# A two-layer streaming encoder on one core: the layer loop and the MLP loop as hardware loops, and as straight code

## The chip, the cores and the metric

The kernel runs on one core of a Trainium2 chip. The metric is the device time of one launch in microseconds (us), median of several runs. Five instruction streams run side by side: TensorE (PE, with weight loads shown apart as PEld), VectorE (DVE), ScalarE (ACT), GpSimd (POOL) and SyncE (SP), which issues the large DMAs. They meet only through semaphores.

## The reference, cut to what matters

All tensors are float32, the sequence has 256 rows, the model width is 2048, and there are two layers. Each does

```
proj = rmsnorm(x) @ w_in                 # 2048 x 4352, split into three head groups
x   += concat(A, B, C) @ w_out           # A chunked attention, B sliding window, C differential attention
x   += relu(rmsnorm(x) @ w_up)**2 @ w_down   # 2048 x 8192 and 8192 x 2048
```

Both layers compute the same with other weights; only a constant of C (`lam_init`) depends on the layer. The MLP is by far the largest part: 512 of the 720 units of weights, of up to 512 KB each.

## The kernel before, in words

**Units.** All weights are streamed once. A unit is a piece of 256 rows by 512 columns of a weight matrix, brought by one DMA on SP's queue into `raw_ring` (8 places). To keep float32 accuracy, each unit is split: ACT writes the rounded part `w_hi` (L611), DVE, or POOL for 17 units of each layer, writes the remainder `w_lo` (L783, L1152). The split parts have 4 places (`AHEAD = 4`): at step s the engines split unit s + 4 while PE works on unit s. PE multiplies each unit with the split activations in three passes, hi x hi, lo x hi, hi x lo: 12 matmuls of 512 columns in a `rows_unit` (L428 to L430), and 24 matmuls of 256 columns in an `up_unit` (L467 to L469).

**Steps.** One layer is 360 steps. Steps 0 to 71 are the projection, with the attention parts put between units by tables of step numbers; then 32 steps of `w_out`; then the MLP: 32 steps of `w_up`, three turns of a loop of 32 `w_down` steps and 32 `w_up` steps, and a last 32 steps of `w_down`. The order is written out by hand in `mix` and `mlp`, once for each engine, and `layer_steps` (L290) runs them in order.

**Loops.** Two loops are hardware loops on every engine that takes part: `Fori(0, DEPTH)` over layers (on PE it is L602, on DVE L1093) and inside it `Fori(0, LOOPS)` over the three turns (L297). Each engine has its own registers, its own branch back and no barrier with the others. Semaphores count up over the whole program, so a wait inside a loop compares with a number worked out from the loop's registers (`Place.at`). Addresses of the weights on SP are worked out in registers too (`snap`). The chain semaphores `dve_chain` and `pool_chain`, by which an engine waits for its own last instruction (`link`), are cleared at the end of each layer. `sp_passed` and `dve_passed` are counted up and waited for by nobody; each holds a wait in front of the instruction behind it.

**Who is needed at a turn's start.** The last unit of a turn is an `up_unit`, the first of the next a `rows_unit` on `ht`. That unit waits for `h_done` (the first half of the activations), for `evicted` of its bank, and for its own split. The same hand-over, in the same words, stands at the loop's entry and at its exit: four places in the two layers have no branch back, four have one.

**Rope.** POOL turns the heads of five projection chunks in each layer (L1136 to L1140); DVE normalises them afterwards (L889) and PE transposes them (L475). In those stretches DVE works through short instructions, each waiting for the one before (L795 to L804), between its splits.

Of the kernel before, what the change touches and what calls it, by code (L numbers as in the profile page):

```python
# [148 lines left out]
def encoder(nc, x_in, norm1_g, w_in, a_qnorm_g, a_knorm_g, a_rel_bias, b_qnorm_g, b_knorm_g, b_sinks, c_qnorm_g,  # L149
            c_knorm_g, c_lambda_q1, c_lambda_k1, c_lambda_q2, c_lambda_k2, c_subln_g, w_out, norm2_g, w_up, w_down,  # L150
            consts, out):
    with ExitStack() as ctx:
# [94 lines left out]
        dve_chain, pool_chain = sem("dve_chain"), sem("pool_chain")  # L247
        stored = sem("stored")

        sp_passed, dve_passed = sem("sp_passed"), sem("dve_passed")  # L250

        H_CHUNKS = 16

        class Place:
# [35 lines left out]
        def layer_steps(eng, l, do_mix, do_mlp):  # L290

            pl = Place(l)
            for s in range(UP0):
                do_mix(pl, s)
            for st in mlp_steps(UP0, ["up"]):
                do_mlp(pl, *st)
            with eng.Fori(0, LOOPS) as i:  # L297
                for st in mlp_steps(LOOP0, ["down", "up"]):
                    do_mlp(Place(l, i), *st)
            for st in mlp_steps(DOWN3, ["down"]):  # L300
                do_mlp(pl, *st)
# [29 lines left out]
        @block.sync  # L331
        def _(sp):
            def load(pl, u, w, width, offset, cols):
                at = sp.snap(offset)

                if u - RAWS in POOL_UNITS:
                    sp.wait_ge(pool_split, pl.at(len(POOL_UNITS), POOL_UNITS.index(u - RAWS) + 1))
                else:
                    sp.wait_ge(split_done, pl.at(VECTOR_SPLITS, vector_splits(u - RAWS + 1) + RAWS, LOOP_UNITS))
                sp.sem_inc(sp_passed, 1)  # L340
                sp.dma_start(raw_ring[:, u % RAWS, :, 0:cols],
                             bass.AP(w.tensor, at, [[width, P], [P * width, 2], [1, cols]])).then_inc(raw_loaded[u % RAWS], 16)

            def load_proj(pl, u, layer):
                chunk, k, cols = proj_or_out(u % UNITS)
                load(pl, u, w_in, IN_W, layer * (D * IN_W) + (k * 2 * P * IN_W + PROJ[chunk][1]), cols)

            def mix(pl, s):
                u = s + FIRST_LOADS
                if u < PU:  # L350
                    load_proj(pl, u, pl.l)
                elif u < UP0:
                    chunk, k, cols = proj_or_out(u)
                    load(pl, u, w_out, D, pl.l * (D * D) + (k * 2 * P * D + (chunk - NPROJ) * CW), cols)
                else:
                    load_up(pl, u, 0, u - UP0)
                if s == 36:
                    sp.wait_ge(ext_stored, 16)
                    at = sp.snap(pl.l * (8 * EXT) + 1 + CHUNK)

                    sp.wait_ge(maxed, pl.at(JOBS, 1))
                    sp.sem_inc(sp_passed, 1)
                    sp.dma_start(bias_t[0:CHUNK, :, CHUNK:SEQ],
                                 bass.AP(ext_dram.tensor, at, [[1, CHUNK], [EXT, 8], [1, SEQ - CHUNK]])).then_inc(bias_loaded, 16)
                    sp.dma_start(bias_t[CHUNK:P, :, :],
                                 bass.AP(ext_dram.tensor, at, [[1, CHUNK], [EXT, 8], [1, SEQ]])).then_inc(bias_loaded, 16)

            def load_up(pl, u, c, k):

                i = 0 if pl.i is None else pl.i  # L370
                col = (c + (0 if u < LOOP0 else 4)) * CW + i * (4 * CW)
                load(pl, u, w_up, D_FF, pl.l * (D * D_FF) + k * 2 * P * D_FF + col, CW)

            def load_down(pl, u, c, k, past=False):
                i = 0 if pl.i is None else pl.i
                row = (c // 4 + (2 * LOOPS if past else 0)) * (D_FF // 8) + k * 2 * P
                load(pl, u, w_down, D, pl.l * (D_FF * D) + i * (2 * (D_FF // 8) * D) + (row * D + (c % 4) * CW), CW)

            def mlp(pl, s, part, buf, c, k, n):

                u = s + FIRST_LOADS
                if part == "up":
                    n = c * UPC + k + FIRST_LOADS
                    if n < 4 * UPC:
                        load_up(pl, u, n // UPC, n % UPC)
                    elif s < LOOP0:
                        load_down(pl, u, 0, n - 4 * UPC)
                    else:
                        load_down(pl, u, 8, n - 4 * UPC)
                else:  # L390
                    n = c * 4 + k + FIRST_LOADS
                    if n < 32:
                        load_down(pl, u, n // 4, n % 4, s >= DOWN3)
                    elif s < DOWN3:
                        load_up(pl, u, 0, n - 32)
                    else:

                        load_proj(pl, u, DEPTH - 1 - pl.l)

            assert DEPTH == 2  # L400
            sp.dma_start(rows[R_G1:R_G1 + DEPTH * KT, :], norm1_g.rearrange("l (k p) -> (l k) p", p=P)).then_inc(g1_loaded, 16)
            load_x(sp, 0)
            sp.dma_start(rows[R_G2:R_G2 + DEPTH * KT, :], norm2_g.rearrange("l (k p) -> (l k) p", p=P)).then_inc(rows_loaded, 16)
            for u in range(FIRST_LOADS):
                load_proj(Place(0), u, 0)
                if u < 3:
                    load_x(sp, u + 1)
            sp.dma_start(par[:, :, SINK:SINK + 16],
                         bass.AP(b_sinks.tensor, 0, [[0, P], [16, DEPTH], [1, 16]])).then_inc(misc_loaded, 16)
            sp.dma_start(const[:, C_MASK:CONSTS], consts[:, C_MASK:CONSTS]).then_inc(const_loaded, 16)  # L410
            for n, g in enumerate((c_qnorm_g, c_knorm_g, b_knorm_g, b_qnorm_g)):
                sp.dma_start(gains[:, :, n, :], bass.AP(g.tensor, 0, [[0, P], [HD, DEPTH], [1, HD]])).then_inc(misc_loaded, 16)
            with sp.Fori(0, DEPTH) as l:
                layer_steps(sp, l, mix, mlp)
            for c in range(4):
                n = CHUNKS - 4 + c

                sp.wait_ge(evicted[n % 2], Place(DEPTH - 1).evictions(n) + 1)
                sp.dma_start(out[0, :, c * CW:(c + 1) * CW].rearrange("(r p) n -> p r n", p=P),
                             x[:, :, c * CW:(c + 1) * CW]).then_inc(stored, 16)  # L420
            sp.wait_ge(stored, 16 * 4)
# [3 lines left out]
        def _(pe):  # L425
# [170 lines left out]
            for k in range(PANELS_BEFORE):  # L596
                pe.wait_ge(x_loaded[k // 2], 16)
                transposes(x_panel(k), start_banks[k])
                if k == 1:
                    pe.wait_ge(rows_loaded, 16 * 4)  # L600
                    pe.transpose(ps_v[:, 0:ROWS], rows, const[0:ROWS, C_ID:C_ID + ROWS]).then_inc(rows_t, 1)
            with pe.Fori(0, DEPTH) as l:  # L602
                layer_steps(pe, l, mix, mlp)


# [1 line left out]
        def _(act):  # L607
# [156 lines left out]
            act.dma_start(ext_dram.rearrange("l h n -> (l h) n"), head_sq[0:DEPTH * 8, 0:EXT]).then_inc(ext_stored, 16)  # L764
            act.wait_ge(lam_dot, 1)
            act.activation(lam[:, :], lam[:, :], ACT.Exp).then_inc(lam_exp, 1)
            with act.Fori(0, DEPTH) as l:
                layer_steps(act, l, mix, mlp)


# [1 line left out]
        def _(dve):  # L772
# [118 lines left out]
            def mask_and_max(pl, j):  # L891

                dve.wait_ge(scored, pl.at(JOBS, j + 1))
                if j == 24:
                    dve.wait_ge(bias_loaded, pl.at(32, 32))
                dve.sem_inc(dve_passed, 1)
                for r, (lo, n) in enumerate(((0, P), (P, SEQ))):
                    if j < 24:
                        col = C_MASK if j < 8 or r == 0 else C_MASKB
                        add = const[:, col + SEQ - n:col + SEQ]  # L900
                    else:

                        add = bass.AP(bias_t[:, :, :].tensor, (j - 24) * SEQ + n - 1, [[8 * SEQ, P], [-1, n]])
                    first = BIG if not 8 <= j < 24 else cur[:, NSINK + j - 8:NSINK + j - 7]
                    last = dve.tensor_tensor_reduce(probs[:, j % 3, lo:lo + n], ps_s[:, lo:lo + n], add, -0.125, first,
                                                    ALU.add, ALU.min, neg_max[:, j, r:r + 1])
                last.then_inc(maxed, 1)
# [181 lines left out]
            for l in range(DEPTH):  # L1089
                link(dve.scalar_tensor_tensor(par[:, l, NLAM:NLAM + 1], lam[:, 2 * l + 1:2 * l + 2], -lam_init(l),  # L1090
                                              lam[:, 2 * l:2 * l + 1], ALU.add, ALU.subtract))
            dve.sem_clear(dve_chain)
            with dve.Fori(0, DEPTH) as l:  # L1093
                links[0] = 0
                layer_steps(dve, l, mix, mlp)
                dve.sem_clear(dve_chain)


        @block.gpsimd
        def _(pool):  # L1100
# [40 lines left out]

            pool.wait_ge(const_loaded, 16)
            pool.wait_ge(misc_loaded, 16 * 5)
            with pool.Fori(0, DEPTH) as l:
                links[0] = 0
                rope_tables(l)
                for c in ROPED:
                    chunk(l, c)
# [1 line left out]
                for n, u in enumerate(POOL_UNITS):  # L1150
                    pool.wait_ge(hi_ready, pl.unit(u + 1))
                    pool.tensor_tensor(w_lo[:, u % AHEAD, :, :], raw_ring[:, u % RAWS, :, :],  # L1152
                                       w_hi[:, u % AHEAD, :, :].bitcast(F32), ALU.subtract).then_inc(pool_split, 1)
                pool.sem_clear(pool_chain)


# [37 lines left out]
```

## Time and profile before

| | |
|---|---|
| Device time, 3 runs | 2210.84, 2211.62 (median), 2215.09 us |
| Profiled execution, span | 2210.4 us (its own time is not given apart from the span) |
| PE busy | 2159.0 us, 98% of the span |
| PE weight loads busy | 1898.4 us |
| DVE, ACT, POOL busy | 1300.5, 990.7, 196.0 us |
| Mean granted TensorE clock | 0.994 of 2.4 GHz |
| Instructions | 36151 |
| Instruction DMA, queues q8 and q14 | 1.87 MB in 114 packets, 0.65 MB in 79 |

How to read it: the median of the runs is 1.2 us above the span of the profiled execution. PE's matmuls overlap in the profile, so their durations add up to more than the pace at which they start: a matmul of 512 columns is shown as 0.39 us and starts 0.23 us behind the last, one of 256 columns is shown as 0.28 us and starts 0.12 us behind. A pause is therefore measured here from start to start, and set against the usual distance. The chain that ended last is 88% PE, 6% DVE, 3% issue and 2% ACT.

### The profile page before, as it was taken

What the parts mean: (1) busy time and instruction counts of PE and PEld (TensorE: products, weight loads), DVE (VectorE), ACT (ScalarE), POOL (GpSimd) and SP (SyncE); (2) the same over time, 40 slices, a digit from 0 to 9 for tenths busy, and PEclk for the clock granted to TensorE, in tenths of its full rate; (3) what the DMA queues carried; (4) which work ended last, traced back from release to release, by engine and by line L of the source; (5) the groups of instructions that cost most, each with busy time, mean ns of one, the idle gap of its engine ahead of it and who ended that gap; (6) DMA issues with size and microseconds to landing.
All of it is one profiled execution on the core that took longest, in us unless ns stands there. A gap on an engine that the chain in (4) does not pass through costs nothing.

```text
span 2210.4 us, 36151 instructions
## 1 busy us (share of the span) xinstructions
PE 2159.0 (98%) x12790; PEld 1898.4 (86%) x12790; DVE 1300.5 (59%) x1737; ACT 990.7 (45%) x1357; POOL 196.0 (9%) x170
## 2 busy tenths in 40 slices
PE   7999999999999999999999999999999999999999
PEld 6777888998998997899878778889989889988987
DVE  7678546555545555555676775465555555555556
ACT  5445545443344343344445455444434434433444
POOL 3223230000000000000012332200000000000000
PEclk9999999999999999999999999999999999999999
DMA  8563345656655655665555433466566556556554
GB/s 263 150 178 112 117 134 182 181 188 193 188 173 191 190 182 169 194 181 188 184 171 177 140 108 129 144 179 184 186 195 182 174 195 186 184 178 191 182 190 152
DMA packets 203809, 384.99 MB, mean 174 GB/s; under 512 B 13310, under 2 KB 20192, under 8 KB 203616
## 3 DMA queue, kind: packets, MB, share of 16 engines
q1 hardware_dynamic: 202816, 382.11, 55.2%
q8 instruction: 114, 1.87, 0.3%
q10 hardware_dynamic: 800, 0.37, 0.1%
q14 instruction: 79, 0.65, 0.1%
HBM read 380.31 MB, written 2.12 MB: 173 GB/s over the span
## 4 chain that ended last, share of the span: by engine, by line
PE 88%; DVE 6%; issue 3%; ACT 2%; DMA 0%; DVEq 0%; SPq 0%; ACTq 0%
PE acc L428 16%; PE acc L430 16%; PE acc L429 16%; PE acc L469 11%; PE acc L468 11%; PE acc L467 11%; DVE w_lo L783 2%; PE ps_t L475 2%; PE ps_s L526 1%; PE ps_s L525 1%; ACT w_hi L611 1%; PE ps_p L540 1%; PE ps_v L556 1%; PE ps_v L557 1%; DVE small L864 0%
## 5 line engine op out<-in xcount | busy, mean ns | idle before, releaser
L783 DVE TENSOR_TENSOR w_lo<-raw_ring,w_hi 128x1024 fp32r<-128x1024 f32 (+1 forms) x690 | 854.7, 1240 | 810.6 <-ACT w_hi L611 806.5
L611 ACT CAST w_hi<-raw_ring 128x1024 fp32r<-128x1024 f32 (+1 forms) x724 | 752.9, 1040 | 1000.5 <-PE acc L430 579.0
L467 PE MATMUL acc<-xt_hi,w_hi 128*128 128x256 f32 x2048 | 580.8, 284 | 0.0
L468 PE MATMUL acc<-xt_lo,w_hi 128*128 128x256 f32 x2048 | 580.6, 283 | 0.0
L469 PE MATMUL acc<-xt_hi,w_lo 128*128 128x256 f32 x2048 | 580.6, 283 | 0.0
L428 PE MATMUL acc<-w_hi,ht_hi 128*128 128x512 f32 x1280 | 505.6, 395 | 12.7 <-DVE w_lo L783 8.8
L430 PE MATMUL acc<-w_hi,ht_lo 128*128 128x512 f32 x1280 | 500.9, 391 | 0.0
L429 PE MATMUL acc<-w_lo,ht_hi 128*128 128x512 f32 x1280 | 500.4, 391 | 0.0
L467 PEld LDWEIGHTS acc<-xt_hi,w_hi 128*128 128x128 f32 x2048 | 393.7, 192 | 0.3
L468 PEld LDWEIGHTS acc<-xt_lo,w_hi 128*128 128x128 f32 x2048 | 393.6, 192 | 0.3
L469 PEld LDWEIGHTS acc<-xt_hi,w_lo 128*128 128x128 f32 x2048 | 393.7, 192 | 0.0
L428 PEld LDWEIGHTS acc<-w_hi,ht_hi 128*128 128x128 f32 x1280 | 241.6, 189 | 65.9 <-DVE w_lo L783 9.4
L430 PEld LDWEIGHTS acc<-w_hi,ht_lo 128*128 128x128 f32 x1280 | 241.3, 189 | 51.1
L429 PEld LDWEIGHTS acc<-w_lo,ht_hi 128*128 128x128 f32 x1280 | 241.8, 189 | 48.8
L428 PE MATMUL acc<-w_hi,xt_hi 128*128 128x512 f32 (+1 forms) x512 | 203.6, 398 | 0.0
L430 PE MATMUL acc<-w_hi,xt_lo 128*128 128x512 f32 (+1 forms) x512 | 195.3, 381 | 0.0
L429 PE MATMUL acc<-w_lo,xt_hi 128*128 128x512 f32 (+1 forms) x512 | 195.0, 381 | 0.0
L428 PEld LDWEIGHTS acc<-w_hi,xt_hi 128*128 128x128 f32 x512 | 98.1, 192 | 26.8 <-issue 9.9
L430 PEld LDWEIGHTS acc<-w_hi,xt_lo 128*128 128x128 f32 x512 | 97.7, 191 | 19.1
L429 PEld LDWEIGHTS acc<-w_lo,xt_hi 128*128 128x128 f32 x512 | 98.2, 192 | 15.9
L1136 POOL TENSOR_TENSOR head_sq<-head_in,rope_s 128x256 f32<-128x256 f32 (+1 forms) x20 | 15.2, 759 | 991.0 <-DVE small L864 991.0
L1152 POOL TENSOR_TENSOR w_lo<-raw_ring,w_hi 128x1024 fp32r<-128x1024 f32 x34 | 81.7, 2404 | 212.9 <-ACT w_hi L611 212.9
(141 smaller groups left out, 1366.2 us busy)
## 6 DMA issues: line engine op xcount, KB each, us to landing
raw_ring<-in_w_up_dram SPq DMA_DIRECT2D x256, 512.0 KB, 3.7
raw_ring<-in_w_down_dram SPq DMA_DIRECT2D x256, 512.0 KB, 3.6
raw_ring<-in_w_in_dram SPq DMA_DIRECT2D x132, 512.0 KB, 3.8
raw_ring<-in_w_out_dram SPq DMA_DIRECT2D x64, 512.0 KB, 3.7
raw_ring<-in_w_in_dram SPq DMA_DIRECT2D x16, 256.0 KB, 2.8
x<-in_x_dram SPq DMA_DIRECT2D x4, 512.0 KB, 8.8
out_dram<-x SPq DMA_DIRECT2D x4, 512.0 KB, 4.0
bias_t<-ext_bias SPq DMA_DIRECT2D x2, 512.0 KB, 8.2
```

The source lines that it names most:

```text
L428: pe.matmul(out_ap, t_hi, m_hi, start=start, stop=False, skip_group_check=True)
L429: pe.matmul(out_ap, t_hi, m_lo, start=False, stop=False, skip_group_check=True)
L430: return pe.matmul(out_ap, t_lo, m_hi, start=False, stop=stop, skip_group_check=True)
L467: pe.matmul(o, hi, xt[0][:, kt, :], start=kt == 0 and f % 2 == 0, stop=False, skip_group_check=True)
L468: pe.matmul(o, hi, xt[1][:, kt, :], start=False, stop=False, skip_group_check=True)
L469: mm = pe.matmul(o, lo, xt[0][:, kt, :], start=False, stop=last, skip_group_check=True)
L475: mm = pe.transpose(bank[:, n * P:(n + 1) * P], b, ident)
L525: pe.matmul(ps_s[:, 0:P], q[lo:lo + HD, b, 0:P], k[lo:lo + HD, kb, 0:P], start=True, stop=True)
L526: pe.matmul(ps_s[:, P:3 * P], q[lo:lo + HD, b, P:2 * P], k[lo:lo + HD, kb, :], start=True, stop=True).then_inc(scored, 1)
L611: act.copy(w_hi[:, u % AHEAD, :, 0:cols], raw_ring[:, u % RAWS, :, 0:cols]).then_inc(hi_ready, 1)
L783: dve.tensor_tensor(w_lo[:, u % AHEAD, :, 0:cols], raw_ring[:, u % RAWS, :, 0:cols], w_hi[:, u % AHEAD, :, 0:cols].bitcast(F32), ALU.subtr ...
L1152: pool.tensor_tensor(w_lo[:, u % AHEAD, :, :], raw_ring[:, u % RAWS, :, :], w_hi[:, u % AHEAD, :, :].bitcast(F32), ALU.subtract).then_inc( ...
```

## The change

The two hardware loops become Python loops, so the program that each engine gets is written out for two layers and three turns. Every semaphore target is then a constant, and so is every weight address. The two semaphores nobody waits for are gone, and the two chain semaphores are no longer cleared. What is computed, the tables of steps, buffers, DMAs and their sizes stay as they are.

```diff
--- before.py
+++ after.py
@@ -247,8 +247,6 @@
         dve_chain, pool_chain = sem("dve_chain"), sem("pool_chain")
         stored = sem("stored")
 
-        sp_passed, dve_passed = sem("sp_passed"), sem("dve_passed")
-
         H_CHUNKS = 16
 
         class Place:
@@ -294,7 +292,7 @@
                 do_mix(pl, s)
             for st in mlp_steps(UP0, ["up"]):
                 do_mlp(pl, *st)
-            with eng.Fori(0, LOOPS) as i:
+            for i in range(LOOPS):
                 for st in mlp_steps(LOOP0, ["down", "up"]):
                     do_mlp(Place(l, i), *st)
             for st in mlp_steps(DOWN3, ["down"]):
@@ -331,15 +329,12 @@
         @block.sync
         def _(sp):
             def load(pl, u, w, width, offset, cols):
-                at = sp.snap(offset)
-
                 if u - RAWS in POOL_UNITS:
                     sp.wait_ge(pool_split, pl.at(len(POOL_UNITS), POOL_UNITS.index(u - RAWS) + 1))
                 else:
                     sp.wait_ge(split_done, pl.at(VECTOR_SPLITS, vector_splits(u - RAWS + 1) + RAWS, LOOP_UNITS))
-                sp.sem_inc(sp_passed, 1)
                 sp.dma_start(raw_ring[:, u % RAWS, :, 0:cols],
-                             bass.AP(w.tensor, at, [[width, P], [P * width, 2], [1, cols]])).then_inc(raw_loaded[u % RAWS], 16)
+                             bass.AP(w.tensor, offset, [[width, P], [P * width, 2], [1, cols]])).then_inc(raw_loaded[u % RAWS], 16)
 
             def load_proj(pl, u, layer):
                 chunk, k, cols = proj_or_out(u % UNITS)
@@ -356,10 +351,8 @@
                     load_up(pl, u, 0, u - UP0)
                 if s == 36:
                     sp.wait_ge(ext_stored, 16)
-                    at = sp.snap(pl.l * (8 * EXT) + 1 + CHUNK)
-
+                    at = pl.l * (8 * EXT) + 1 + CHUNK
                     sp.wait_ge(maxed, pl.at(JOBS, 1))
-                    sp.sem_inc(sp_passed, 1)
                     sp.dma_start(bias_t[0:CHUNK, :, CHUNK:SEQ],
                                  bass.AP(ext_dram.tensor, at, [[1, CHUNK], [EXT, 8], [1, SEQ - CHUNK]])).then_inc(bias_loaded, 16)
                     sp.dma_start(bias_t[CHUNK:P, :, :],
@@ -410,7 +403,7 @@
             sp.dma_start(const[:, C_MASK:CONSTS], consts[:, C_MASK:CONSTS]).then_inc(const_loaded, 16)
             for n, g in enumerate((c_qnorm_g, c_knorm_g, b_knorm_g, b_qnorm_g)):
                 sp.dma_start(gains[:, :, n, :], bass.AP(g.tensor, 0, [[0, P], [HD, DEPTH], [1, HD]])).then_inc(misc_loaded, 16)
-            with sp.Fori(0, DEPTH) as l:
+            for l in range(DEPTH):
                 layer_steps(sp, l, mix, mlp)
             for c in range(4):
                 n = CHUNKS - 4 + c
@@ -599,7 +592,7 @@
                 if k == 1:
                     pe.wait_ge(rows_loaded, 16 * 4)
                     pe.transpose(ps_v[:, 0:ROWS], rows, const[0:ROWS, C_ID:C_ID + ROWS]).then_inc(rows_t, 1)
-            with pe.Fori(0, DEPTH) as l:
+            for l in range(DEPTH):
                 layer_steps(pe, l, mix, mlp)
 
 
@@ -764,7 +757,7 @@
             act.dma_start(ext_dram.rearrange("l h n -> (l h) n"), head_sq[0:DEPTH * 8, 0:EXT]).then_inc(ext_stored, 16)
             act.wait_ge(lam_dot, 1)
             act.activation(lam[:, :], lam[:, :], ACT.Exp).then_inc(lam_exp, 1)
-            with act.Fori(0, DEPTH) as l:
+            for l in range(DEPTH):
                 layer_steps(act, l, mix, mlp)
 
 
@@ -893,7 +886,6 @@
                 dve.wait_ge(scored, pl.at(JOBS, j + 1))
                 if j == 24:
                     dve.wait_ge(bias_loaded, pl.at(32, 32))
-                dve.sem_inc(dve_passed, 1)
                 for r, (lo, n) in enumerate(((0, P), (P, SEQ))):
                     if j < 24:
                         col = C_MASK if j < 8 or r == 0 else C_MASKB
@@ -1089,11 +1081,8 @@
             for l in range(DEPTH):
                 link(dve.scalar_tensor_tensor(par[:, l, NLAM:NLAM + 1], lam[:, 2 * l + 1:2 * l + 2], -lam_init(l),
                                               lam[:, 2 * l:2 * l + 1], ALU.add, ALU.subtract))
-            dve.sem_clear(dve_chain)
-            with dve.Fori(0, DEPTH) as l:
-                links[0] = 0
+            for l in range(DEPTH):
                 layer_steps(dve, l, mix, mlp)
-                dve.sem_clear(dve_chain)
 
 
         @block.gpsimd
@@ -1141,8 +1130,7 @@
 
             pool.wait_ge(const_loaded, 16)
             pool.wait_ge(misc_loaded, 16 * 5)
-            with pool.Fori(0, DEPTH) as l:
-                links[0] = 0
+            for l in range(DEPTH):
                 rope_tables(l)
                 for c in ROPED:
                     chunk(l, c)
@@ -1151,7 +1139,6 @@
                     pool.wait_ge(hi_ready, pl.unit(u + 1))
                     pool.tensor_tensor(w_lo[:, u % AHEAD, :, :], raw_ring[:, u % RAWS, :, :],
                                        w_hi[:, u % AHEAD, :, :].bitcast(F32), ALU.subtract).then_inc(pool_split, 1)
-                pool.sem_clear(pool_chain)
 
 
 # ---- launch ----
```

**PE at the turn's end and start.** On PE, at the end of the loop's body, the last matmuls of the turn are followed by a count, a branch back to the body's first row, and there by waits of their own; before the change:

```order
L467 MATMUL acc<-xt_hi,w_hi 128x256
L468 MATMUL acc<-xt_lo,w_hi 128x256
L469 MATMUL acc<-xt_hi,w_lo 128x256
L297 REGISTER_ALU
L297 COMPARE_AND_BRANCH
```

The body's first rows, to which it jumps back:

```order
L442 ISA [waits h_done]
L436 ISA [waits evicted1]
L428 MATMUL acc<-w_hi,ht_hi 128x512 [waits split_done]
L429 MATMUL acc<-w_lo,ht_hi 128x512
L430 MATMUL acc<-w_hi,ht_lo 128x512
```

The same place now, PE between the first and the second turn:

```order
L460 MATMUL acc<-xt_hi,w_hi 128x256
L461 MATMUL acc<-xt_lo,w_hi 128x256
L462 MATMUL acc<-xt_hi,w_lo 128x256
L421 MATMUL acc<-w_hi,ht_hi 128x512 [waits split_done,evicted1,h_done]
L422 MATMUL acc<-w_lo,ht_hi 128x512
L423 MATMUL acc<-w_hi,ht_lo 128x512
```

Nothing stands between the two matmuls any more; the three waits are the same. In PE's whole list, 4179 rows with four branches and two compare-and-branch rows became 12145 rows with one branch at each end.

**DVE in a rope stretch.** On DVE, behind the chain of short instructions (`small`, 16 values to a partition) for the first projection chunk, before:

```order
L795 TENSOR_SCALAR small<-small 128x16 [waits summed]
L796 TENSOR_SCALAR small<-small 128x16 [waits dve_chain]
L797 TENSOR_SCALAR small<-small 128x16 [waits dve_chain]
L782 REGISTER_ALU [waits dve_chain]
L783 TENSOR_TENSOR w_lo<-raw_ring,w_hi 128x1024 [waits hi_ready]
```

and now:

```order
L788 TENSOR_SCALAR small<-small 128x16 [waits summed]
L789 TENSOR_SCALAR small<-small 128x16 [waits dve_chain]
L790 TENSOR_SCALAR small<-small 128x16 [waits dve_chain]
L776 TENSOR_TENSOR w_lo<-raw_ring,w_hi 128x1024 [waits hi_ready,dve_chain]
L776 TENSOR_TENSOR w_lo<-raw_ring,w_hi 128x1024 [waits hi_ready]
```

The register instruction that held the chain's wait is gone and its wait stands with the split. DVE had 289 register rows (21 of them with a wait for `dve_chain`), ACT 309, PE 320 and SP 170; all are gone.

## Rows read from the trace of the kernel before

**Rows 1.** Spans and granted clock of the core; the page's busy times.

```profile
core 0: 2210.4 us, clock 0.994
...
PE 2159.0 (98%) x12790; PEld 1898.4 (86%) x12790; DVE 1300.5 (59%) x1737; ACT 990.7 (45%) x1357; POOL 196.0 (9%) x170
```

**Rows 2.** PE's waits: engine, line, releaser: us in total, times, longest.

```profile
PE ps_t L475 <- DVE head_in L889: 13.5, 6, 3.9
PE acc L428 <- DVE w_lo L783: 8.8, 3, 3.2
```

**Rows 3.** PE's timeline, branch back 840: start us, us, instruction [idle, releaser].

```profile
836.47 0.28 PE L469 MATMUL acc<-xt_hi,w_lo 128*128 128x256 f32 x1
840.71 0.79 PE L428 MATMUL acc<-w_hi,ht_hi 128*128 128x512 f32 x1 [3.96 <-issue]
```

**Rows 4.** The same at the other three branches back of the MLP loop.

```profile
653.93 0.28 PE L469 MATMUL acc<-xt_hi,w_lo 128*128 128x256 f32 x1
657.25 0.49 PE L428 MATMUL acc<-w_hi,ht_hi 128*128 128x512 f32 x1 [3.04 <-DVE w_lo L783]
...
1749.57 0.28 PE L469 MATMUL acc<-xt_hi,w_lo 128*128 128x256 f32 x1
1753.05 0.49 PE L428 MATMUL acc<-w_hi,ht_hi 128*128 128x512 f32 x1 [3.21 <-DVE w_lo L783]
...
1932.24 0.28 PE L469 MATMUL acc<-xt_hi,w_lo 128*128 128x256 f32 x1
1935.03 0.49 PE L428 MATMUL acc<-w_hi,ht_hi 128*128 128x512 f32 x1 [2.52 <-DVE w_lo L783]
```

**Rows 5.** PE's timeline where layer 0 enters the MLP loop, no branch back.

```profile
474.71 0.28 PE L469 MATMUL acc<-xt_hi,w_lo 128*128 128x256 f32 x1
474.83 0.40 PE L428 MATMUL acc<-w_hi,ht_hi 128*128 128x512 f32 x1
475.06 0.40 PE L429 MATMUL acc<-w_lo,ht_hi 128*128 128x512 f32 x1
```

**Rows 6.** DVE's timeline at that entry, then at the branch back at 654.

```profile
476.11 1.23 DVE L783 TENSOR_TENSOR w_lo<-raw_ring,w_hi 128x1024 fp32r<-128x1024 f32 x1 [1.66 <-ACT w_hi L611]
...
655.32 1.23 DVE L783 TENSOR_TENSOR w_lo<-raw_ring,w_hi 128x1024 fp32r<-128x1024 f32 x1 [1.65 <-ACT w_hi L611]
```

**Rows 7.** ACT's timeline at the branch back at 654.

```profile
654.24 1.04 ACT L611 CAST w_hi<-raw_ring 128x1024 fp32r<-128x1024 f32 x1 [1.83 <-PE acc L469]
655.19 1.02 ACT L724 ACTIVATE head_sq<-acc 128x1024 f32<-128x1024 f32 x1
```

**Rows 8.** DMA queues: at the branch back (654.2 to 655.4), then 660 to 830.

```profile
q8 instruction: 1, 0.02, 4.8%
...
q8 instruction: 9, 0.15, 0.4%
```

**Rows 9.** Stretches: us, busy PE, PEld, DVE, ACT, POOL, PEclk, DMA, GB/s.

```profile
840.71:846.79 6.08, 6.08 (x14) 4.79 (x15) 0.00 (x0) 0.56 (x1) 0.00 (x0) 0.51 0.23 81
1935.03:1939.00 3.97, 3.97 (x11) 3.11 (x11) 0.00 (x0) 0.00 (x0) 0.00 (x0) 0.57 0.43 143
660.00:830.00 170.00, 170.00 (x1088) 155.49 (x1087) 93.95 (x85) 70.70 (x68) 0.00 (x0) 1.00 0.59 184
```

**Rows 10.** The same columns, behind one of PE's pauses in a rope stretch.

```profile
62.00:65.50 3.50, 3.50 (x12) 2.90 (x11) 1.26 (x2) 0.59 (x1) 0.00 (x0) 0.56 0.65 182
```

**Rows 11.** PE's timeline at the branch back of the layer loop.

```profile
1112.32 0.39 PE L430 MATMUL acc<-w_hi,ht_lo 128*128 128x512 f32 x1
1113.33 0.49 PE L428 MATMUL ps_s<-w_hi,xt_hi 128*128 128x512 f32 x1 [0.62 <-DVE w_lo L783]
```

**Rows 12.** DVE's timeline in the first rope stretch.

```profile
53.12 0.66 DVE L804 SCALAR_TENSOR_TENSOR small<-small 128x16 f32<-128x16 f32 x1
53.90 2.29 DVE L783 TENSOR_TENSOR w_lo<-raw_ring,w_hi 128x1024 fp32r<-128x1024 f32 x1
```

**Rows 13.** POOL's timeline beside it.

```profile
53.83 1.29 POOL L1138 TENSOR_TENSOR head_in<-head_in,rope_c 128x512 f32<-128x512 f32 x1
```

## The prediction

> **What bounds the kernel now.** I read the busy times first. PE is busy for 2159.0 us of a span of 2210.4 us, DVE for 1300.5 and ACT for 990.7 [rows 1]. The reader is to see one engine that never has much to wait for, and four that follow it. So an edit is worth what it takes from PE's pauses or from the time in which PE runs at its lower clock, and nothing else. Second, PE's waits by releaser [rows 2]: the largest is for the heads that DVE normalises in the rope stretches (13.5 us in 6 waits), then 8.8 us in 3 waits put down to DVE's split, at the line of the first matmul of a `rows_unit`; one more wait there, of 3.96 us, is put down to "issue" [rows 3]. Third, the timeline of PE at those four: all stand where the MLP loop branches back, two in each layer [rows 3, 4]. Fourth, the same hand-over where there is no branch, as a control [rows 5]. Last, the clock in the stretches behind the pauses [rows 9], and the layer loop's own branch [rows 11].
>
> **Whose pause it is.** From the last matmul of a turn to the first of the next, start to start, PE takes 3.32, 4.24, 3.48 and 2.79 us [rows 3, 4]. Where layer 0 enters the loop, the same two matmuls with the same waits stand 0.12 us apart [rows 5]; the exit and layer 1's entry and exit, three more places, look the same. DVE's split, which the trace names as releaser at three of the four, also ends behind the hand-over at the entry (476.11 + 1.23 = 477.34, where PE has gone on at 474.83), and PE does not wait for it there: it belongs to a unit three steps later [rows 5, 6]. So it was merely the last thing to happen before PE went on. ACT crosses its own branch back with no idle time (654.24 + 1.04 us, next start 655.19) [rows 7]. On PE something else is added: just in this pause one block of instructions is fetched on queue q8 [rows 8]. In the 170 us from 660 to 830 nine such blocks arrive and PE is busy for all 170.00 us [rows 8, 9]. Blocks in a row are therefore free, a jump back to one that is no longer there is not. I read the pause as PE's fetch after the branch, which straight code does not have.
>
> [...]
>
> **The change, part by part.**
>
> 1. *The four branches back of the MLP loop go.* The pauses are 3.32 + 4.24 + 3.48 + 2.79 = 13.83 us, and 4 x 0.12 = 0.48 us stay as the usual distance [rows 5]: **13.35 us**. What is late next is nothing for a long time: with the pause gone PE goes on with units whose splits were made up to three steps ahead, as at the entry.
>
> 2. *The lower clock behind two of them.* After the pause at 840 the granted clock of 840.71 to 846.79 is 0.51, after the one at 1935 it is 0.57 for 3.97 us [rows 9]: mostly 1.2 GHz instead of 2.4. In the first, 13 matmuls of 512 columns start in 6.08 us, in the second 10 in 3.97 us; at the usual 0.23 us each [rows 5] they would take 2.99 and 2.30. That is 3.09 + 1.67 = **4.76 us**. Before both, PE had stood still for some 3 to 4 us, and in the two other pauses of that kind no low clock followed, so it hangs on the pause and goes with it.
>
> 3. *The layer loop's branch back.* From 1112.32 to 1113.33 is 1.01 us against 0.23 [rows 11, 5]: **0.78 us**. PE's fetch was evidently done early here.
>
> 4. *Register instructions.* Each engine computes a target beside its running instruction; where the engine is late or PE is far ahead that is hidden: PE's matmuls start at their usual distance all through 660 to 830 [rows 9]. They show only where DVE's chain of short instructions hands over to a split, as in a rope stretch: 53.12 + 0.66 = 53.78, next start 53.90, so 0.12 us of hand-over [rows 12]. A plain hand-over is not free either, so a saving lies between 0 and 0.12 us each. There are 21 such places per layer, 42 in all: 0 to 5 us. Most have no wait of PE behind them. I take 0.08 us for 8 of them, those in front of PE's waits for DVE: **0.6 us**.
>
> 5. *Rope stretches, below nothing.* DVE's split takes 2.29 us while POOL works beside it (L1138 begins at 53.83, the split at 53.90) [rows 12, 13], against 1.23 us elsewhere [rows 6]. The two engines take turns, and a shift by a tenth of a microsecond can move one split in or out of POOL's shadow: up to 1.06 us in either direction in each of ten chunks. The trace of before shows no such shift, and I have no reason for a sign: 0, with both ends kept.
>
> 6. *SP, the dummy semaphores, the cleared chains.* Loads are 4 units ahead and PE is not waiting for a load anywhere in the body. 0. If that cover were gone, a saved tenth per load would be a gain, not a loss.
>
> 7. *Straight code is longer.* The number of instructions run does not rise, so the number of blocks fetched does not either: the loop's body already went past block after block [rows 8]. 0.
>
> Sum: 13.35 + 4.76 + 0.78 + 0.6 = 19.5 us. Against the profiled span of 2210.4 us that is 2190.9; the median of the runs, 2211.62 us, is 1.2 us above the span, and 2211.6 - 19.5 = **2192 us**.
>
> **Own range of that case.** Four other pauses of PE stay, two in each layer, with a low clock behind them for some 3.4 us, of which one is shown [rows 10]. The four pauses of [rows 3, 4] were followed by a loss of 0, 3.09, 0 and 1.67 us, with no order in it that I can use, and everything after 654 now comes earlier by up to 16 us. A clock of one half for 3.4 us costs 1.7 us, so each pause in layer 1 may come out 1.7 us better, or up to 1.4 us worse (3.09 less 1.7) than now. With the 0 to 5 us of part 4 and a few shifts of part 5: 2187 to 2198 us.
>
> **Rivals.**
>
> *The split was the releaser after all.* The trace says so at three of four places. Then PE would go on as soon as the split is done: at 656.55 instead of 657.25, a gain of 0.70 us [rows 4, 6]. At the other pauses I know the releaser only by its name, and if they are alike the gain is 4 x 0.70 + 0.78 = 3.6 us, the clock stays as it is: 2208 us, which is within 0.2%. Against it stands the control [rows 5, 6], and the one pause the trace could not put down to DVE [rows 3]. I give it 5 in 100.
>
> *Rope stretches get worse.* All ten chunks lose 1.06 us on one split, and half of PE's longer pauses get a low clock behind them: 10.6 us off the gain, 2203 us. For it: the two engines do slow each other [rows 12, 13]. Against it: it needs the same sign ten times. 6 in 100.
>
> *Straight code starves the fetch: slower.* PE now streams its whole program, about a hundred blocks, from memory with nothing to fall back on. If the fetch of the next block were exposed in part, the point from which it decides is 19.5 / 100 = 0.2 us a block; at 0.5 us a block the program would be 50 us longer less the gain: 2242 us. For it: a fetch that is not ahead costs 3 us [rows 3, 4]. Against it: nine blocks in 170 us with PE never idle [rows 8, 9], in code that is straight over a whole turn. 3 in 100.
>
> *More than forecast.* Pauses in the rope stretches shrink as well (13.5 us are waited there [rows 2]) and the low clock behind them goes: 2184 us, 4 in 100.
>
> *The change doesn't take the branches out.* The order of PE's rows now has a branch only at each end, so this has no share.
>
> **How the numbers follow.** The forecast's own case has 82 in 100 and gives 2192 us. A measurement of this kernel can tell a difference of about 0.2%, 4.4 us, from none. Faster by more than that (under 2207.2): the forecast, the worse rope stretches, the extra gain, about 0.91. Within it: the releaser case and an edge, 0.06. Slower: 0.03. For the range I leave out the lower case and the slower one in part: 2187 to 2199 us.
>
> **What would show each step right or wrong.** Parts 1 and 3: PE's start-to-start distance at the four turns' ends and between the layers is 0.12 and 0.23 us, as at [rows 5], and no wait at the first matmul of a `rows_unit` is left above 0.3 us. If pauses of 2 us or more stand there with a DVE split behind them, the first rival holds. Part 2: the granted clock is at 2.4 GHz throughout both MLPs, and low only behind the rope stretches' pauses. Part 4 and 5: PE's waits for DVE's heads add up to 13.5 us give or take 3. Part 7: instruction fetches are about as many as before, and PE has no idle time at them in the MLP. The prediction is wrong if the MLP is not about 10 us shorter in layer 0 and 8 in layer 1, or if the time lost or won lies mostly in the first 200 us of a layer.

## The result, and the profile after

| | before | after |
|---|---|---|
| Device time, median | 2213.25 us (4 runs, 2210.84 to 2215.09) | 2193.17 us (4 runs, 2191.94 to 2197.43) |
| Profiled execution: time, span | span 2210.4 us | 2191.94 us, span 2190.1 us |
| Mean granted TensorE clock | 0.994 | 0.997 |
| Instructions | 36151 | 31018 |

The ratio is 0.9913 (95% interval 0.9900 to 0.9925): 20.1 us less. The forecast was 2192 us, 19.5 us less than the median of three runs that it started from (2211.62 us). The profiled execution after is the fastest of the four; the slowest of them, 2197.43 us, has a granted clock of 0.994 and no profile.

PE's hand-over from the first to the second turn of the MLP loop in layer 0 (start us, us, instruction), which answers to [rows 4], first pair, and then the one between the layers, which answers to [rows 11]:

```profile
651.78 0.28 PE L462 MATMUL acc<-xt_hi,w_lo 128*128 128x256 f32 x1
651.90 0.40 PE L421 MATMUL acc<-w_hi,ht_hi 128*128 128x512 f32 x1
...
1099.86 0.39 PE L423 MATMUL acc<-w_hi,ht_lo 128*128 128x512 f32 x1
1100.09 0.39 PE L421 MATMUL ps_s<-w_hi,xt_hi 128*128 128x512 f32 x1
```

The 3.32 us have become 0.12, the 1.01 us between the layers 0.23. The other three hand-overs read 0.12 as well. So the stretch from one to the next is the same length in all six turns, 179.22 us; three of them after (length, busy times of PE, PEld, DVE, ACT, POOL, clock, DMA share, GB/s):

```profile
472.56:651.78 179.22, 179.22 (x1154) 164.26 (x1153) 98.06 (x88) 74.58 (x72) 0.00 (x0) 1.00 0.61 188
651.78:831.00 179.22, 179.22 (x1154) 164.28 (x1153) 98.08 (x88) 74.61 (x72) 0.00 (x0) 1.00 0.60 188
831.00:1010.22 179.22, 179.22 (x1154) 164.25 (x1153) 98.07 (x88) 74.61 (x72) 0.00 (x0) 1.00 0.60 188
```

and the same three turns of layer 0 before:

```profile
474.71:653.93 179.22, 179.22 (x1155) 164.26 (x1153) 98.08 (x88) 74.76 (x72) 0.00 (x0) 1.00 0.61 188
653.93:836.47 182.54, 179.50 (x1155) 164.32 (x1153) 98.08 (x88) 74.76 (x72) 0.00 (x0) 1.00 0.59 185
836.47:1022.73 186.26, 182.30 (x1154) 166.37 (x1153) 98.08 (x88) 74.77 (x72) 0.00 (x0) 0.98 0.58 181
```

The reader is to see that the first turn, which no branch back precedes, already took 179.22 us, that the second is longer by the pause and its restart (3.32 us: the pause exceeds the usual distance by 3.20, and the first matmul behind it holds up the next by 0.1), and the third by pause and low clock (7.04 us, clock 0.98). Taking the same marks through the whole execution:

| From, to (before; after) | before | after | less |
|---|---|---|---|
| start to the MLP loop of layer 0 (474.71; 472.56) | 474.71 | 472.56 | 2.15 |
| its three turns | 548.02 | 537.66 | 10.36 |
| last 32 steps, layer 1's attention, to its MLP loop (1570.34; 1557.85) | 547.61 | 547.63 | -0.02 |
| its three turns | 545.46 | 537.66 | 7.80 |
| to the end | 94.60 | 94.59 | 0.01 |

That is 20.3 us of span, and 18.16 us of it lie in the six turns. The layer loop's branch is in the third row: 0.78 us.

PE's waits after (us in total, times, longest), which answer to [rows 2]:

```profile
PE ps_t L468 <- DVE head_in L882: 11.6, 6, 3.5
...
PE ps_p L533 <- DVE probs_t L918: 4.8, 2, 2.4
PE ps_s L518 <- DVE neg_max L897: 3.8, 5, 0.9
```

The waits at the first matmul of a `rows_unit` are gone from the list. Those for DVE's heads are 1.9 us shorter. Before, the two others read

```profile
PE ps_p L540 <- DVE probs_t L926: 5.0, 2, 2.5
...
PE ps_s L525 <- DVE neg_max L905: 3.1, 4, 1.3
```

so the three together fell from 21.6 to 20.2 us. With 18.16 us in the turns and 0.78 us between the layers this makes up the 20.3 us; the low clock outside the MLP took as much as it gave (below). Fetches on q8 fell a little, from 114 to 101. It is PE's queue: they are 106 in E3 below, where PE's code alone is changed, and 114 in E4, where PE's alone is not.

```profile
q8 instruction: 101, 1.65, 0.3%
```

### The profile page after: what moved, and what is told of

Same layout as the page of the kernel before. It is cut to its first block, busy times and chain, and to the rows that moved or that the text cites. A ratio compares the mean times of both kernels' runs of the same rounds, so it can differ in the third digit from the quotient of the medians.

```text
span 2190.1 us, 31018 instructions
## 1 busy us (share of the span) xinstructions
PE 2154.4 (98%) x12790; PEld 1895.0 (87%) x12790; DVE 1301.6 (59%) x1737; ACT 989.5 (45%) x1357; POOL 196.7 (9%) x170
## 4 chain that ended last, share of the span: by engine, by line
PE 91%; DVE 6%; ACT 1%; SPq 1%; issue 0%; DMA 0%; DVEq 0%; ACTq 0%
PE acc L421 17%; PE acc L423 17%; PE acc L422 17%; PE acc L462 11%; PE acc L461 11%; PE acc L460 11%; DVE w_lo L776 3%; PE ps_t L468 2%; PE ps_s L519 1%; PE ps_s L518 1%; PE ps_p L533 1%; PE ps_v L549 1%; PE ps_v L550 1%; ACT w_hi L604 1%; DVE small L795 0%
```

## The experiments

Each kernel was timed beside the kernel before on the same chip, which read 2213.21, 2210.35 and 2211.29 us in the three groups (E1 to E4, E5 to E8, E9 to E11). Each ratio is to the kernel before, with its 95% interval. "Straight" is a Python loop, "looped" the hardware loop. The edits are shown in short.

**E1, E2: one of the two loops.**

```diff
 # E1: the MLP loop straight on every engine, the layer loop looped
-            with eng.Fori(0, LOOPS) as i:
+            for i in range(LOOPS):
 # E2: the layer loop straight on every engine, the MLP loop looped
-            with pe.Fori(0, DEPTH) as l:            # and so on sp, act, dve, pool
+            for l in range(DEPTH):
```

> The MLP loop is straight on every engine, the layer loop stays a hardware loop. My theory (the pause is PE's own fetch after the branch back, the low clock comes from the pause): PE goes from turn to turn in 179.2 us at all four places, the gain over the kernel before is 18.1 us of the change's 20, so about 2195 us; the 0.8 us between the layers stays. Rival (the gain comes from constant targets on all engines and not from the branches): well under 18 us, since half the code still counts in registers.

> The layer loop is written out on every engine, the MLP loop stays a hardware loop of three turns. My theory: the four pauses at PE's branch back stay, 2.7 to 4.2 us each, some with the low clock behind them; only the 0.8 us between the layers goes, so 2210 to 2213 us. Rival (code that is longer or shorter matters, not the branch): the time falls clearly below 2208.

E1: 2194.49 us, ratio 0.9911 (0.9894 to 0.9927), all turns 179.22 us. E2: 2211.26 us, ratio 0.9987 (0.9977 to 0.9996); the pauses are there, 3.61, 3.02, 2.87 and 2.70 us start to start, and between the layers PE's distance is 0.23 us. The first of E2's:

```profile
657.10 0.28 PE L481 MATMUL acc<-xt_hi,w_lo 128*128 128x256 f32 x1
660.71 0.49 PE L440 MATMUL acc<-w_hi,ht_hi 128*128 128x512 f32 x1 [3.33 <-DVE w_lo L795]
```

Nearly the whole gain is the MLP loop's. E2's gain of 2 us is small but outside its interval. The layer loop's branch is 0.78 us of it, and PE waits 11.5 us for DVE's heads there instead of 13.5 (see E6); the profiled execution is only 0.8 us shorter than the one before (2209.6 against 2210.4 us), so what each brings is not told apart.

**E3, E4: one engine's loop.**

```diff
 # E3: only PE has the MLP loop straight;  E4: all but PE have it straight
+def turns(eng, name, straight, n):
+    if name in straight:
+        for v in range(n):
+            yield v
+    else:
+        with eng.Fori(0, n) as v:
+            yield v
-            with eng.Fori(0, LOOPS) as i:
+            for i in turns(eng, name, INNER, LOOPS):   # E3: INNER = ['pe'], E4: all others
```

> Only PE has the MLP loop straight; ACT, DVE and SP branch back as before, with register targets. My theory (PE's own fetch): the whole 18 us come, 2195 us, and the first matmul of a turn starts 0.12 us behind the last of the turn before. Rival (PE waits for DVE's split or ACT, delayed by their own branches): the four pauses stay in good part, 2205 us or more.

> The reverse: ACT, DVE and SP have the MLP loop straight, PE branches back as before. My theory: the four pauses of 2.7 to 4.2 us stay whole, with a low clock behind none to all of them, 2208 to 2216 us. Rival (the others' branches hold PE up): the pauses shrink to under 1 us, about 2195 us.

E3: 2194.46 us, ratio 0.9915 (0.9892 to 0.9938), all six turns 179.22 us. E4: 2213.23 us, ratio 0.9996 (0.9986 to 1.0006), pauses of 3.30, 3.60, 3.35 and 2.69 us. E4's first pause on PE:

```profile
657.93 0.28 PE L481 MATMUL acc<-xt_hi,w_lo 128*128 128x256 f32 x1
661.23 0.49 PE L440 MATMUL acc<-w_hi,ht_hi 128*128 128x512 f32 x1 [3.02 <-DVE w_lo L795]
```

DVE is straight there, and the trace still names its split as the releaser. That rules out the first rival: neither DVE's nor ACT's nor SP's MLP loop holds PE up. PE's own branch is enough, and needed.

**E5: the branch kept, with a branch hint.**

```diff
 # on PE's MLP loop only; every other loop as before
-            with eng.Fori(0, LOOPS) as i:
+            with eng.bass.Fori(0, LOOPS, engines=OrderedEngineSet([eng.engine]), hint_back_edge=True) as i:
```

The hint is one instruction at the top of each turn, on PE's sequencer (PEldq). Six were run, and the whole program has just six instructions more than before (36157 against 36151). In the view of that line: count, shortest/median/longest ns, first and last start:

```profile
L143 PEldq BRANCH_PREFETCH_HINT  x6: 36/36/50, 473.3 to 1915.9; - x6
```

> The kernel before, every loop kept, with one instruction more on PE: a branch hint at the top of each turn of its MLP loop, which names the branch back so that its target's block can be fetched in time. My theory (the pause is the fetch of that block, not the branch): the four pauses of 2.7 to 4.2 us shrink to under 0.6 us, no low clock behind them, about 2195 us; the pauses in the rope stretches stay as before (13.5 us for DVE's heads). Rival (the branch itself empties PE's queue, or register targets are late after it): the pauses stay above 2 us and the time at 2212 us.

2192.64 us, ratio 0.9919 (0.9902 to 0.9936): as fast as straight code, with all registers, branches and loops in place. PE's timeline at the second branch back, and the two turns beside it:

```profile
833.67 0.28 PE L485 MATMUL acc<-xt_hi,w_lo 128*128 128x256 f32 x1
833.79 0.40 PE L444 MATMUL acc<-w_hi,ht_hi 128*128 128x512 f32 x1
```

```profile
654.45:833.67 179.22, 179.22 (x1155) 164.25 (x1153) 98.07 (x88) 74.79 (x72) 0.00 (x0) 1.00 0.60 188
833.67:1012.89 179.22, 179.22 (x1155) 164.23 (x1153) 98.07 (x88) 74.79 (x72) 0.00 (x0) 1.00 0.60 188
```

The 4.24 us of [rows 3] are 0.12 with a taken branch in between. The trace also keeps a record of the compare-and-branch itself, which PE's timeline leaves out. Here it is at the first and the second branch back before, at the layer loop's branch before, and at the first branch back with the hint:

```profile
L297 PEldq COMPARE_BRANCH  x1: 4714/4714/4714, 652.0 to 652.0; - x1
...
L297 PEldq COMPARE_BRANCH  x1: 5630/5630/5630, 834.5 to 834.5; - x1
...
L602 PEldq COMPARE_BRANCH  x1: 4302/4302/4302, 1108.6 to 1108.6; - x1
...
L143 PEldq COMPARE_BRANCH  x1: 393/393/393, 652.5 to 652.5; - x1
```

The reader is to see when they start and end. The first starts at 652.01, 1.92 us before the last matmul of the turn (653.93), and ends at 656.72; PE's next matmul starts 0.53 us behind that end. The same 1.92 and 0.53 us stand at all four branches back, while DVE's split, the releaser that the trace names, ends 0.70, 1.61, 0.86 and 0.17 us before PE goes on. So each pause is the branch's length less 1.92 plus 0.53, which is 3.3, 4.2, 3.5 and 2.8 us for branches of 4.71, 5.63, 4.88 and 4.18 us. With the hint the branch is over at 652.92 (652.53 + 0.39), and the last matmul of the turn starts at 654.45.

The fetch is seen beside the branch. In each of the four stretches from a branch's start to its end before (652.01 to 656.72, 834.55 to 840.18, 1747.64 to 1752.52, 1930.32 to 1934.50) there is one instruction packet on q8, and so there is in the four of E2 and the four of E4; in the layer loop's, of 4.30 us, there are two. At the first of the four:

```profile
q8 instruction: 1, 0.02, 1.2%
```

With the hint there is none during the four branches (0.35 to 0.39 us each), and none from 643.2 to 654.4. So the long branches go with a fetch, and one hint took the whole price away here (4.71 us of branch became 0.39). That the branch waits for that packet is my reading of the two; how the hint works no trace shows.

**E9, E10: branches to a target at hand.**

```diff
 # all straight; on PE, between the turns (E10: 16 in place of 4)
+                with pe.Fori(0, 4) as _turn:
+                    pe.sem_inc(near, 1)
```

> All straight, and on PE, at the four places where turns met, a tiny loop of 4 turns (one register instruction that also counts up a semaphore, and a branch back): three taken branches to a target a few instructions back, at each place. My theory (a branch whose target is at hand costs a few tenths at most, the fetch was the price): PE's distance at those places is under 1.2 us, probably near 0.5, and the total at most 4 us above all straight. Rival (a taken branch as such stops PE for 2.7 us or more): 8 us and more at each place, over 2225 us.

> The same with 16 turns: 15 taken branches at each place. The slope against the run with 4 gives the price of one taken branch to a target at hand. My theory: 0.1 to 0.3 us each, so PE's distance there is 1.5 to 4.5 us. Rival: far above 10 us at each place.

E9: 2196.14 us (2191.24 to 2197.66), ratio 0.9935 (0.9919 to 0.9952); the distances on PE are 0.12 to 0.17 us, its turns 179.27 to 179.36 us. The profiled execution is the fastest of the four, at a clock of 0.997; the three others, some 5 us slower, are at 0.994, and where they lost it was not profiled. E10: 2226.24 us (2 runs), ratio 1.0069 (1.0049 to 1.0089), distances of 6.41 to 6.45 us. One place of each, E9 and then E10:

```profile
653.42 0.28 PE L465 MATMUL acc<-xt_hi,w_lo 128*128 128x256 f32 x1
653.59 0.47 PE L424 MATMUL acc<-w_hi,ht_hi 128*128 128x512 f32 x1
```

```profile
656.53 0.28 PE L465 MATMUL acc<-xt_hi,w_lo 128*128 128x256 f32 x1
662.97 0.76 PE L424 MATMUL acc<-w_hi,ht_hi 128*128 128x512 f32 x1 [6.17 <-issue]
```

(6.44 - 0.17) / 12 is 0.52 us a turn of the tiny loop, for its three instructions. The branch alone is recorded with 0.21 us (median; 0.08 us where it is not taken), E9:

```profile
L588 PEldq COMPARE_BRANCH  x16: 76/208/237, 651.8 to 1915.4; - x16
```

E10 missed: I had expected 0.1 to 0.3 us a turn and at most 4.5 us in all. But 16 x 0.52 = 8.3 us show as a pause of only 6.3, and 4 x 0.52 = 2.1 us as one of 0.05: about 2 us of the branches were hidden here, which is the 1.92 us read above. It is not a fixed time. The layer loop's branch, which stands behind matmuls of 512 columns, starts 3.75 us before the last of them (1108.57, 1112.32). In both places 16 or 17 matmuls still start after the branch has begun, so PE's sequencer was ahead by about that many matmuls, and the wider ones hid more (3.75 us against 1.92).

**E8: a pause without a branch.**

```diff
 # all straight; PE, at the start of the second and third turn
+                    if s == LOOP0 and pl.i:
+                        unit_is_split(pl, s + 3)
```

> All straight, but at the start of the second and third turn PE also waits for the split of the unit three steps on, which DVE finishes about 2.6 us after PE's last matmul: a pause of 2.7 us without a branch and without a fetch at four places, so 10.3 us of waiting. My theory (the low clock comes from PE standing still, whatever the reason): the total is 10.3 us plus half the time at the low clock, which may follow none, some or all of the pauses: 2203 to 2211 us. Rival (the low clock belongs to the branch or fetch): exactly 10.3 us, and no low clock in the MLP in any profile.

2207.45 us, ratio 0.9984 (0.9975 to 0.9994): 14.3 us above the changed kernel's median. The four distances are 2.77 us each, 10.6 us more than 0.12 in all; after the second of each layer the clock falls, for 3.4 us. The profiled spans are 15.7 us apart (2205.8 and 2190.1): 10.6 of pauses, 3.4 of low clock behind two of them, and 1.7 of one more low stretch of 3.4 us at the rope. PE's timeline there, and the two turns and the low stretch:

```profile
835.24 0.28 PE L462 MATMUL acc<-xt_hi,w_lo 128*128 128x256 f32 x1
838.01 0.47 PE L421 MATMUL acc<-w_hi,ht_hi 128*128 128x512 f32 x1 [2.50 <-issue]
```

```profile
653.29:835.24 181.95, 179.46 (x1155) 164.28 (x1153) 98.07 (x88) 74.60 (x72) 0.00 (x0) 1.00 0.60 185
835.24:1018.82 183.58, 181.09 (x1154) 165.41 (x1153) 98.07 (x88) 74.59 (x72) 0.00 (x0) 0.99 0.58 184
839.30:842.90 3.60, 3.60 (x11) 2.78 (x10) 0.00 (x0) 0.57 (x1) 0.00 (x0) 0.53 0.41 133
```

A turn behind a pause of 2.77 us is longer by 2.73, or by 4.36 where the granted clock falls behind it (0.53 from 839.30 to 842.90). So the low clock did not need a branch: it came behind two of the four pauses of 2.77 us in which PE stood still, and not behind the other two. In the other direction, none of the profiles without pauses there (after, E1, E3, E5, E6, E7, E9, E11) shows a low clock in the MLP.

**E6, E7: who shortens the rope stretches.**

```diff
 # E6: DVE looped in both loops, all others straight;  E7: POOL looped, all others straight
-            for l in range(DEPTH):                # dve in E6, pool in E7
+            with dve.Fori(0, DEPTH) as l:
```

Both also keep the two semaphores nobody waits for, as E1 to E5 and E11 do, and the looped engine keeps its chain semaphore's clearing.

> DVE keeps both hardware loops and its register instructions, PE, ACT, SP and POOL are straight. My theory: PE waits for DVE's heads 13.5 us again instead of 11.6, since DVE's hand-overs are 0.12 us again and its split runs in POOL's shadow for 2.29 us; the MLP stays at 179.2 us a turn; 2194 to 2196 us. Rival (POOL's own straight code shifts the rope stretches): 11.6 us stay.

> POOL keeps its layer loop and register instructions, the four other engines are straight. My theory (DVE's hand-over decides the rope stretches): PE waits 11.5 us for DVE's heads, as with all straight, 2193 us. Rival (POOL decides): 13.5 us.

E6: 2195.74 us, ratio 0.9932 (0.9916 to 0.9949). E7: 2195.06 us, ratio 0.9929 (0.9913 to 0.9946). PE's waits in E6, then in E7:

```profile
PE ps_t L487 <- DVE head_in L901: 13.4, 6, 4.0
...
PE ps_p L552 <- DVE probs_t L938: 3.8, 2, 2.6
PE ps_s L537 <- DVE neg_max L917: 3.5, 5, 1.5
```

```profile
PE ps_t L487 <- DVE head_in L901: 11.4, 6, 3.4
...
PE ps_p L552 <- DVE probs_t L938: 4.8, 2, 2.4
PE ps_s L537 <- DVE neg_max L917: 3.6, 4, 0.9
```

This repeats in all profiles: where DVE's layer loop is looped (before, E1, E3, E4, E5, E6) PE waits 13.4 or 13.5 us for the heads, where it is straight (after, E2, E7 to E11) 11.4 to 11.6. DVE's timeline in the changed kernel shows how, against [rows 12], and POOL's against [rows 13]:

```profile
52.54 0.67 DVE L797 SCALAR_TENSOR_TENSOR small<-small 128x16 f32<-128x16 f32 x1
53.24 1.72 DVE L776 TENSOR_TENSOR w_lo<-raw_ring,w_hi 128x1024 fp32r<-128x1024 f32 x1
```

```profile
53.13 0.74 POOL L1126 TENSOR_TENSOR head_sq<-head_in,rope_s 128x256 f32<-128x256 f32 x1
53.95 2.16 POOL L1127 TENSOR_TENSOR head_in<-head_in,rope_c 128x512 f32<-128x512 f32 x1
```

The hand-over is 53.24 - (52.54 + 0.67) = 0.03 us instead of 0.12. DVE's split now starts before POOL's long instruction, not just behind its start, and takes 1.72 us instead of 2.29; POOL's takes 2.16 instead of 1.29. E6 has the lengths of before (2.29 and 1.29 us), E7 those of after (1.72 and 2.15 us), so DVE's code decides the order; that it does so by the 0.09 us is read from the rows and was not tried by itself. But the sum of the three waits is 20.7 us in E6 and 19.8 in E7: half of what the heads win is waited for elsewhere, and the medians of E6 and E7 cannot be told apart. In E1 and E3, with DVE's layer loop looped, the three add up to 20.2 us (13.5, 3.8 and 2.9), no more than in the changed kernel. A gain in time from DVE's straight code is therefore not shown.

**E11: the two causes and nothing else.** Every engine but DVE looped, the hint of E5 on PE, DVE straight.

> The smallest edit that the results so far point to: all engines but DVE keep their loops, PE's MLP loop carries the branch hint, and DVE alone is straight in both loops. My theory (two causes make the whole gain: PE's fetch and DVE's hand-over): PE at 179.2 us a turn, 11.5 us of waiting for DVE's heads, 0.7 us left between the layers, 2191 to 2194 us, no different from all straight. Rival (other engines' registers count too): 2195 us or more and 13.5 us of waiting.

2192.38 us, ratio 0.9922 (0.9906 to 0.9939); all turns 179.22 us, 11.5 us of waiting for the heads. It cannot be told from the change (2193.17 us) or from E5 (2192.64 us), which has the hint alone: the first cause carries the time, the second shows in PE's waits only. No version beats the changed kernel by more than a measurement can tell.

## Why the prediction was right

*Parts 1 and 2, 18.1 us.* Measured in the six turns: 18.16 us. E3 and E4 show that the pause is PE's own (0.12 us at the turns in E3, 2.69 to 3.60 in E4). E5 shows that it goes with the long branch (4.71 us became 0.39, with no packet on q8 during it), E9 that three taken branches to a target at hand cost 0.05 us at most, E8 that the low clock comes with a pause that has no branch (3.4 us of it behind two of four). The forecast's low clock is a granted clock of 0.50: before, from 842.15 to 845.99, matmuls of 512 columns start 0.427 us apart (nine in 3.84 us), or 1.2 columns a ns. The 1.2 and 2.4 GHz are an estimate from that: one column a cycle at 0.50, and twice as much at 1.00.

*Part 3, 0.78 us.* 1.01 us became 0.23. The size was as forecast; E2 has 0.23 too, and E3 and E5, with the layer loop looped, 0.95 and 0.96. The reason given, that PE's fetch was done early, was wrong: the branch took 4.30 us, as long as the others, but 3.75 us of it lay under matmuls of 512 columns.

*Part 4, 0.6 us.* The hand-over was read rightly (0.12 us) but mis-sized in its effect: I priced it by itself. DVE and POOL change their order, and PE's waits for the heads are 1.9 us less.

*Part 5, 0, with both ends kept.* The shift existed. Of the 1.9 us, 0.5 are waited for in two other places, which leaves 1.4 us for parts 4 and 5 together against 0.6 forecast. Since E1 and E3 come to the same 20.2 us of waits by another way, these 1.4 us are not firmly DVE's. That the two engines take turns is borne out by their lengths: each is its own plus what the other's instruction has left, less 0.14 to 0.16 us. DVE's 1.23 us become 2.29 with 1.22 us of POOL's left (before) and 1.72 with 0.63 left (after, POOL's from 53.13 to 53.87); POOL's 1.29 us become 2.16 with 1.01 us of DVE's left (after).

*Part 6, 0.* E3, with SP's loop and registers as before, takes 2194.46 us, E1, with SP's MLP loop straight, 2194.49.

*Own range.* The low clock behind the rope stretches moved as feared. Before, layer 0 had two such stretches of 3.4 us, after it has one; in layer 1 one of the two became twice as long:

```profile
1267.90:1274.70 6.80, 6.74 (x17) 4.90 (x18) 4.49 (x17) 3.28 (x11) 0.00 (x0) 0.50 0.38 125
```

That is 1.7 us won in the first stretch of the table and 1.7 us lost in the third, which is why the third shows no gain although the layer branch went and waits shrank. The two cancel, so the total came out within about 1 us by some luck: the sum of the sure terms was 18.9 us, the rest is what these small ones left.

*Part 7 and the starving rival.* 101 fetches instead of 114, and PE busy for all 179.22 us of each turn: nothing starves.

*The rival of DVE's split.* It fell with E4: DVE straight, pauses whole. The name in brackets was of an event that came last before PE went on, not of what held it: the distance from it to PE's start varies from 0.17 to 1.61 us, that from the branch's end is 0.53 us each time.

*What stays open.* Why equal pauses are followed by a low clock at one place and not at another was not settled. Of the sixteen pauses of 2.7 to 4.2 us in before, E2, E4 and E8, eight were, and the length alone does not decide it: the one of 2.70 us in E2 was, the one of 3.48 us in before was not. All four of 6.4 us in E10 were. Nor was the effect of the two dropped semaphores tried by itself; E11 has them and is as fast, so it is small.

## What to carry to other kernels

Look for a hand-over that the program makes both with and without a branch back: the difference is the branch's price, and here it gave 18 of 20 us (the low clock behind the pauses included) before anything was run. When the busiest engine's branch back is long in the trace (4.2 to 5.6 us here, with an instruction packet in each), try writing out that engine's loop alone, or hinting its branch: here this got nearly all of the gain (E3 2194.46 us, E5 2192.64 us, against 2193.17 with all straight), and the other engines' loops could stay. Look for the branch's own record on the sequencer: its start and end say how much of it was hidden. And a releaser named by a trace is a candidate only: find the same releaser at a place where nobody waited for it.

## What the runs showed of the hardware that I had not expected

- PE's sequencer began its branch with 16 or 17 matmuls still to start: 1.92 us at 256 columns, 3.75 us at 512 (before). 2.1 us of tiny branches cost 0.05 us (E9), 8.3 us cost 6.3 (E10).
- So the layer loop's branch of 4.30 us cost 0.78 us behind matmuls of 512 columns, and an MLP loop's of 4.18 us cost 2.67 us behind matmuls of 256 (before).
- With one branch hint a compare-and-branch of 4.71 us became one of 0.39 us (E5).
- With 0.09 us less in DVE's hand-over DVE and POOL ran in another order, and both engines' instructions had other lengths (2.29 to 1.72 us, 1.29 to 2.16 us).
- Two pauses of the same 2.77 us, 182 us apart, had no low clock and 3.4 us of low clock behind them (E8).
